# A hybrid SSD, attention and mixture-of-experts layer: group products moved ahead of attention, half as many partition sums, both ends of the expert stage rearranged

## The reference

```
cb     = einsum("bclgn,bcsgn->bcgls", cc, bc)            # C.B, one product per group
scores = cb[:, :, :, None] * decay                       # decay = exp(a_cs[l] - a_cs[s]), causal
y      = einsum("bcgrls,bcsgrp->bclgrp", scores, xdt) + d_skip * xs
yg     = y * silu(z)
yg     = yg * rsqrt(mean(yg * yg over the 512 columns of a group) + EPS) * norm_w
```

```
h = h + (g_ssd * y_ssd @ w_ssd_out + g_mla * y_mla @ w_o) @ w_out
h = h + moe_ffn(rms_norm(h))          # top 4 of 32 experts, clamped SwiGLU, 1024 -> 2048 -> 1024
out = rms_norm(h)[:, 16:]
```

## Time and profile before

| | |
|---|---|
| median of 3 runs (lowest, highest) | 1380.6 us (1380.5, 1382.89) |
| the profiled execution: time, span | 1382.37, 1380.6 us |
| mean granted TensorE clock | 0.994 of full |
| TensorE busy, weight loads | 1319.2 us (96%), 637.0 us (46%) |
| VectorE, ScalarE, GpSimd busy | 457.8, 319.6, 73.3 us |
| moved by DMA | 461.83 MB, mean 335 GB/s |
| dense part, join, SSD loop | to 191, to 199, to 282 us |
| gates and output products, routing | to 394, to 441 us |
| experts, tail behind the last weights | to 1364, to 1380.6 us |

### The profile page before, as it was taken

How to read it: one execution, slowest core, us unless ns; L and a number is a source line. 1 busy time by engine, 2 the same in 40 slices (tenths; PEclk the granted TensorE clock), 3 DMA queues, 4 the chain that set the end, 5 groups by cost and what they waited for, 6 DMA issues and landing times.

```text
span 1380.6 us, 18645 instructions
## 1 busy us (share of the span) xinstructions
PE 1319.2 (96%) x7121; PEld 637.0 (46%) x7121; DVE 457.8 (33%) x1185; ACT 319.6 (23%) x649; POOL 73.3 (5%) x83
## 2 busy tenths in 40 slices
PE   7999999999999999999999999999999999999995
PEld 5858888899964333333322222222222223333331
DVE  5838879888523211121111121111112111121112
ACT  3537767654311111011100110110010011111001
POOL 0000004422211000000000000000000000000000
PEclk9999999999998999999999999999999999999999
DMA  6333133334976999999999999999999999999995
GB/s 247 132 122 122 62 123 122 123 144 181 375 318 226 420 417 416 417 418 418 418 418 418 417 416 419 419 418 418 417 417 417 418 415 418 418 418 418 417 416 225
DMA packets 77426, 461.83 MB, mean 335 GB/s; under 512 B 6864, under 2 KB 6864, under 8 KB 41152
## 3 DMA queue, kind: packets, MB, share of 16 engines
q1 hardware_dynamic: 76624, 458.67, 82.0%
q0 software_dynamic: 752, 2.49, 0.5%
HBM read 460.09 MB, written 1.05 MB: 334 GB/s over the span
## 4 chain that ended last, share of the span: by engine, by line
PE 66%; SPq 18%; DMA 12%; issue 2%; DVE 1%; ACT 1%; ACTq 0%; DVEq 0%
PE bank L1308 62%; DMA ring<-w_dram 12%; SPq L407 9%; SPq L374 8%; PE bank L1643 1%; PE bank L1637 1%; DMA ring<-slabs_dram 1%; PE bank L1659 1%; PE bank L1505 1%; PE bank L1427 0%; DVE split L889 0%; SPq L395 0%; PE bank L1447 0%; PE bank L1443 0%; PE bank L1444 0%
## 5 line engine op out<-in xcount | busy, mean ns | idle before, releaser
L1308 PE MATMUL bank<-ring,work 128*64 128x512 f32 (+5 forms) x2264 | 551.7, 593 | 34.5 <-DMA ring<-w_dram 31.8
L1308 PE MATMUL bank<-work 128*64 128x512 f32 (+8 forms) x2200 | 431.2, 546 | 6.5 <-issue 2.2
L1308 PEld LDWEIGHTS bank<-ring,work 128*64 128x64 f32 (+2 forms) x2264 | 175.2, 141 | 361.0 <-issue 266.6
L1308 PEld LDWEIGHTS bank<-work 128*64 128x64 f32 (+4 forms) x2200 | 145.2, 143 | 259.2 <-issue 245.6
L1256 DVE COPY work<-bank 128x256 f32<-128x256 f32 x32 | 13.6, 425 | 495.9 <-PE bank L1659 495.9
L1308 PE MATMUL bank<-hn_hi,split 128*128 128x256 f32 (+1 forms) x896 | 172.9, 288 | 0.0
L1308 PEld LDWEIGHTS bank<-hn_hi,split 128*128 128x128 f32 x896 | 141.4, 189 | 0.6
L1308 PE MATMUL bank<-hn_lo,split 128*128 128x256 f32 (+1 forms) x448 | 127.3, 284 | 0.0
L1230 DVE TENSOR_SCALAR work<-bank 128x256 f32<-128x256 f32 x64 | 24.2, 419 | 275.5 <-PE bank L1308 275.5
L889 DVE TENSOR_TENSOR split<-ring,split 128x1024 fp32r<-128x1024 f32 x80 | 99.7, 1248 | 27.2 <-ACT split L547 26.8
L742 ACT ACTIVATE work<-bank 128x512 f32<-128x512 f32 x32 | 19.1, 598 | 333.3 <-PE bank L1308 333.3
(11 more groups left out here) (250 smaller groups left out, 909.7 us busy)
## 6 DMA issues: line engine op xcount, KB each, us to landing
ring<-w_dram SPq DMA_DIRECT2D x256, 1024.0 KB, 21.6
work<-w_dram SPq DMA_DIRECT2D x128, 1024.0 KB, 20.1
ring<-slabs_dram SPq DMA_DIRECT2D x23, 2048.0 KB, 7.4
ring<-slabs_dram SPq DMA_DIRECT2D x2, 1152.0 KB, 5.2
ring<-slabs_dram SPq DMA_DIRECT2D x1, 1536.0 KB, 12.0
ring<-slabs_dram SPq DMA_DIRECT2D x1, 1280.0 KB, 8.7
work<-x_dram POOLq DMA_DIRECT2D x2, 512.0 KB, 16.0
out_dram<-work SPq DMA_DIRECT2D x4, 256.0 KB, 2.5
```

The costliest lines, as they stand in the source:

```text
L1308: return pe.matmul(o, lhsT, rhs, start=start, stop=stop)
```

## The change

Seven edits, on five engines. (1) The group products stand between query units 2 and 3, their masking on VectorE ahead of the rotation of the queries, and `CBm` lies elsewhere; the SSD loop starts without them, the rows and transposes of chunk 1 come behind unit z 1, and ScalarE reads z 0 ahead of the loop. (2) The squares of two chunks are added on VectorE (`ysum_of`), and `gsum_of` runs on the sums, 8 times. (3) Logits are made in halves; the transposes of the third part of h1 stand ahead of the rest of the last `w_out` part, one copy of h1 ahead of the last half of the logits; the normalizer takes the first half's sum ahead of time. (4) The bias products of `up` stand on their own (`up_bias`), ahead of the wait for the gathered rows; in expert 0 they stand ahead of its transposes, behind the wait for the count. (5) For the last expert the transposes stand inside `down` of the one before, and `down` uses another bank and buffer with the scatter inside. (6) TensorE, ScalarE read the count ahead of their last expert's work; the branch stays in its place. (7) The stores of the second block are issued by ScalarE.

```diff
-        CBm = w(R + 4096, GROUPS * DECAY).rearrange("p (g t) -> p g t", g=GROUPS)
+        CBm = w(7424, GROUPS * DECAY).rearrange("p (g t) -> p g t", g=GROUPS)
...
-        ysq = w(R + 11008, 512).rearrange("p (i t) -> p i t", i=2)
+        ysq = w(R + 4096, 1024).rearrange("p (i t) -> p i t", i=4)
...
+        scat_last = w(13312, SEQ)
+        actT_last = xgT
...
         @block.sync
-                sp.wait_ge(y1_ready, n + 1)
-                sp.dma_start(out[P:2 * P, n * 512:(n + 1) * 512], fin[:, 1, n * 512:(n + 1) * 512]).then_inc(y_out, 16)
...
         @block.scalar
             def squares_of(c):
                 a.wait_ge(y2_ready, c + 1)
-                if c >= 2:
-                    a.wait_ge(gsum_done, c - 1)
-                a.activation(ysq[:, c % 2, :], y2T[:, c, :], ACT.Square, scale=0.5).then_inc(ysq_ready, 1)
+                if c >= 4:
+                    a.wait_ge(gsum_done, c // 2 - 1)
+                a.activation(ysq[:, c % 4, :], y2T[:, c, :], ACT.Square, scale=0.5).then_inc(ysq_ready, 1)
...
+            z_of(0)
             for c in range(NX):
                 if c + 1 < NX:
                     diff2_of(c + 1)
                 if c:
                     squares_of(c - 1)
...
+                    z_of(c)
                 if c + 1 < NX:
                     exp_decay(c + 1)
                 hi_of(PZ + c + 3)
...
             xn_copy(0, 1)
+            xn_copy(1, 0)
             top_weights(0)
             square_half(1, 1)
-            xn_copy(1, 0)
             xn_copy(1, 1)
...
+            a.wait_ge(count_ready, 1)
             expert_round(FIRST)
-            a.wait_ge(count_ready, 1)
-            cm = a.value_load(cmax_i[0:1, 0:1], min_val=0, max_val=SEQ)
-            with a.If(cm > SLOTS):
+            with a.If(cm[0] > SLOTS):
...
+            for n in range(2):
+                a.wait_ge(y1_ready, n + 1)
+                a.dma_start(out[P:2 * P, n * 512:(n + 1) * 512], fin[:, 1, n * 512:(n + 1) * 512]).then_inc(y_out, 16)
...
         @block.vector
+            for g in range(GROUPS):
+                cb_of(g)
+
             d.wait_ge(proj_read, U["q", 7] + 1)
...
+            def ysum_of(c):
+
+                d.wait_ge(ysq_ready, c + 1)
+                d.tensor_tensor(ysq[:, c % 4 - 1, :], ysq[:, c % 4 - 1, :], ysq[:, c % 4, :], ALU.add).then_inc(ysum_ready, 1)
...
             sc_of(0)
+            lo_of(PZ + 2)
             for c in range(NX):
                 if c + 1 < NX:
                     diff_of(c + 1)
                     xdt_of(c + 1)
-                lo_of(PZ + c + 2)
+                if c:
+                    lo_of(PZ + c + 2)
...
-                if c and c % CHUNKS_PER_GROUP == 0:
+                if c % 2 == 0 and c:
+                    ysum_of(c - 1)
+                if c > CHUNKS_PER_GROUP and c % CHUNKS_PER_GROUP == 1:
                     var_group(c // CHUNKS_PER_GROUP - 1)
+            ysum_of(NX - 1)
...
+            def first_half(b):
+                d.wait_ge(h1_squared, 2 * b + 1)
+                link(d.tensor_scalar(ssh[:, b:b + 1], ssh4[:, b, 0:1], 0.5 / D, 0.5 * EPS, ALU.mult, ALU.add))
+
             def rstd_block(b):
                 d.wait_ge(h1_squared, 2 * (b + 1))
-                link(d.tensor_tensor(ssh[:, b:b + 1], ssh4[:, b, 0:1], ssh4[:, b, 1:2], ALU.add))
-                rstd_col(rsh[:, b:b + 1], ssh[:, b:b + 1], D, EPS, rsn_ready)
+                link(d.scalar_tensor_tensor(ssh[:, b:b + 1], ssh4[:, b, 1:2], 0.5 / D, ssh[:, b:b + 1], ALU.mult, ALU.add))
+                rsqrt_col(rsh[:, b:b + 1], ssh[:, b:b + 1], rsn_ready)
...
         @block.tensor
+            def chunk_products():
+                pe.wait_ge(conv_fin, 8)
+                pe.wait_ge(kpeT_ready, 2)
+                for g in range(GROUPS):
+                    ps = bank[4 + g]
+                    for (t0, n), (lo, at) in zip(BLOCKS, DECAY_AT):
+                        last = mm(ps[0:n, at:at + SEQ - lo], BT[:, g, t0:t0 + n], CT[:, g, lo:SEQ])
+                    last.then_inc(cb_done, 1)
...
                     last.then_inc(proj_done, 1)
+                    if i == 2:
+                        chunk_products()
...
-            pe.wait_ge(pv_read, KD)
-            for g in range(GROUPS):
-                ps = bank[4 + g]
-                for (t0, n), (lo, at) in zip(BLOCKS, DECAY_AT):
-                    last = mm(ps[0:n, at:at + SEQ - lo], BT[:, g, t0:t0 + n], CT[:, g, lo:SEQ])
-                last.then_inc(cb_done, 1)
...
+            def gsum_of(i):
+
+                pe.wait_ge(ysum_ready, i + 1)
+                if i and i % 2 == 0:
+                    pe.wait_ge(gsum_read, i // 2)
+                mm(bank[7][:, 0:SEQ], ones[:, :], ysq[:, i % 2 * 2, :], i % 2 == 0, i % 2 == 1).then_inc(gsum_done, 1)
...
             for c in range(NX):
-                if c + 1 < NX:
+                if 0 < c < NX - 1:
                     acum_of(c + 1)
                     xtr_of(c + 1)
...
+                if c == 0:
+                    acum_of(1)
+                    xtr_of(1)
+                    pe.wait_ge(pv_read, KD)
...
-                if c:
-                    gsum_of(c - 1)
+                if c >= 3 and c % 2:
+                    gsum_of(c // 2 - 1)
...
             wout_unit(1, 1, range(0, 3))
-            logits(0)
+            logits(0, 0)
+            logits(0, 1)
+            h1_transposes(1, 0)
             wout_unit(1, 1, range(3, KD)).then_inc(wout_done, 1)
-            h1_transposes(1, 0)
+            logits(1, 0)
             h1_transposes(1, 1)
-            logits(1)
...
             keep_h1(0, 0)
+            logits(1, 1)
             keep_h1(0, 1)
...
+            def up_bias(t):
                 pe.wait_ge(bsel_ready, t + 1)
...
                     pe.wait_ge(up_read, t + 1)
+                    up_bias(t + 1)
                     up(t + 1, pair, odd, between)
...
+                    if gathers:
+                        down(t)
+                    else:
+                        pe.wait_ge(scat_ready, t + 1)
+                        down(t, between=lambda: last_transposes(t + 1))
...
                 gather(t0)
-                gather_trans(t0)
...
                     pe.wait_ge(bias_in, 64)
                     pe.wait_ge(count_ready, 1)
+                up_bias(t0)
+                gather_trans(t0)
                 up(t0, pair0, 0, first_between)
...
-                act_transposes(t0 + E - 1)
-                scatter(t0 + E - 2)
-                hot_transposes(t0 + E - 1)
-                down(t0 + E - 1)
+                if r is FIRST:
+                    cm.append(pe.value_load(cmax_i[0:1, 0:1], min_val=0, max_val=SEQ))
+                pe.wait_ge(up_read, t0 + E)
+                down(t0 + E - 1, 4, actT_last, lambda: scatter(t0 + E - 2))
...
-            with pe.If(cm > SLOTS):
+            with pe.If(cm[0] > SLOTS):
```

128 lines of the change are left out of this document (71 added, 57 removed).

## The result

The changed kernel takes **1372.23 us** in the median (1372.12 to 1372.85, four runs); the kernel before, on the same chip, 1380.59 (1380.5 to 1382.89). The ratio is 0.9935, with a 95% interval of 0.9922 to 0.9947: 8.4 us faster, where 6.9 were forecast. The two profiled executions lie 9.5 us apart (1382.37 and 1372.85, spans 1380.6 and 1371.1).

The account below looks back on a forecast made before the run. The expert weight stream was taken to bound the kernel, movable only in its start and the tail behind it. Terms 1.1 + 3.5 + 1.4 + 0.9 = 6.9 us off the 1380.6 median gave 1373.7 us, range 1368.5 to 1378.0.

Parts of the forecast that it names:

- C: Routing before expert 0: positions start 3.5 us earlier, 3.35 left, less 1.95 for a slower gather: 1.4 us won.
- rival (a): Routing and expert 0: the granted clock stays up through gather and first k step, worth 5.0, total 1370.2; chance 0.25.
- What bounds the kernel: Expert weight stream, 447 to 1362 us at 417 GB/s: only its start and the tail behind it can move.
- A: Join of attention and SSD: moving the C·B products removes waiting around them, 1.1 us won, bounds 0 and 1.9.
- The sign given for it: SSD loop: the unit of chunk 2 would start about 3.1 us later than now (4.16 - 1.1).
- B: SSD loop: eight partition sums fewer save TensorE 5.0 us, VectorE takes back 1.5: 3.5 us won, bounds -1.2 and 5.0.
- VectorE becomes the slower of the two: SSD loop: VectorE needs 5.15 us a chunk, TensorE 4.96; 0.19 a chunk, 2.5 us over some 13 chunks.
- Rival (b): SSD loop: VectorE takes back all that the eight sums gave, total 1377.2; chance 0.14.
- rival (d): SSD loop: VectorE's additions wait in a ring through ScalarE and TensorE, 12.4 us lost, total 1386.1; chance 0.04.
- I expect the lower level on the gather: Expert 0: after a TensorE wait the clock falls on the gather, which goes from 1.94 to 3.9 us.
- D: Tail behind the last weights: count read earlier, so the branch starts 0.9 earlier: 0.9 us won, bounds 0.2 and 1.9.
- The stores on ScalarE and the steps between experts: Outputs issued by ScalarE: 0, within 0.3 us; bias products ahead of the gathered rows' wait between experts: nothing.

Follow-up runs that it names:

- more_adds: The changed kernel with four more unread VectorE additions of squares ahead of each of its eight real ones: median 1383.5 us.
- before_fill: The kernel before, with eight unread matrix products put into TensorE's two waits of the routing stage: median 1380.5 us.
- no_ends: The changed kernel with the first expert's order, the count's read, the last expert's transposes and bank, and ScalarE's stores as before: median 1374.3 us.
- no_routing: The changed kernel with the routing stage in the old order, the first expert's order left as changed: median 1377.0 us.
- near_scatter: The changed kernel with TensorE's last scatter in a branch of its own ahead of the one that skips the further rounds: median 1372.8 us.
- no_products_move: The changed kernel with the C·B products, their masking, the tanh order of z and the SSD loop's start as before: median 1376.5 us.

## Why the prediction was right, point by point

The total held (1373.7 forecast, 1372.2 measured, inside 1368.5 to 1378.0), but with one term far off, one close by luck and the others close. The parts of the profiled pair come to 10.65 us, not 6.9. That the medians show 8.4 of them has two causes outside the argument: the changed kernel was 1.17 us late from its first stretch, and the two profiled executions stand 1.8 and 0.6 us above their medians. The range held C's error because it was drawn to take in rival (a).

- **What bounds the kernel: right.** The stream moved with its first reload and kept its rate.
- **A, 1.1 forecast: 1.05 measured**, and 1.06 when undone. The sign given for it, a unit of chunk 2 that starts 3.1 us later, contradicts the term: by its own numbers it starts at 191.43 + 4.16 + 7.20 = 202.79, which is 1.1 earlier than 203.93. It came 1.05 earlier behind the latent transposes.
- **B, 3.5 forecast: 3.5 in the profiled pair** (4.0 in the loop and 0.3 of sums behind it, less the wait of 0.77). In six further profiles with the additions, a second wait near 272 us (0.24 to 0.73) and slightly longer loops leave 2.2 to 2.8, so that the exact 3.5 is luck: of the seven, that profile has the fewest long masked decays. The forecast put the meetings with GpSimd into its lower bound only (at each addition); in these profiles they come at the masked decay, and their number goes with the price. The step "VectorE becomes the slower of the two" was right in its effect and wrong in its place: no wait for it is in the loop, which ran at 4.98 us a chunk, against 4.96 by the forecast's sum for TensorE. The backlog shows at the loop's end, where VectorE also has the roots to make. Rival (b) was the same mechanism, carried too far; rival (d) didn't appear: more_adds, with 1.7 us of additions for two chunks, is the only kernel that ends near the time of before.
- **C, 1.4 forecast: 6.0 measured.** The step that failed is "I expect the lower level on the gather": the gather ran at 2.4 GHz, and so did everything through the first k step. That is rival (a), priced at 5.0. Term by term: positions 4.45 (3.5 forecast), gather no slower (-1.95 forecast), first k step 1.25 (nothing forecast), between the positions and the k step 0.3 (-0.15 forecast for the count's wait). The forecast got the positions' 3.5 us by putting the copies at 2.4 GHz, and didn't say how much of it is the clock. before_fill shows that it is three quarters of what was measured: the positions end 4.45 us sooner behind the logits after the change (the second block's mask products start 12.62 behind, against 17.07: 435.58, right behind the row of 435.21, less 418.51), and 3.35 of that is there with the old order and the fill (13.72).
- **D, 0.9 forecast: 0.8 by the means** of all profiles, 0.1 in the profiled pair, where the stream of the changed kernel happened to be slower. By the wait behind ScalarE's copy it is 0.7 in the pair (1.53 and 0.82) and 1.0 by the means (1.78 and 0.81). The branch took 3.75 us, not 3.4.
- The stores on ScalarE and the steps between experts: nothing, as forecast. From the last scatter's start to the end it is 11.9 us before and after, and in no_ends; the stream has 417 GB/s in both.
- The chances: 0.86 for faster is a little high by their own sum, 0.50 + 0.25 + 2/3 of 0.14 = 0.84.

The terms of the profiled pair add up: 1.05 + 3.5 + 6.0 + 0.1, less the 1.17 that the changed kernel was late by from its first stretch, is 9.5. Without any fall of the clock the parts are worth 1.05 + 2.2 to 3.5 + 1.0 + 0.8, or 5 to 6.4 us; the rest is the clock.

**Open:** what decides in an execution whether the clock falls. The old order fell in both of its profiles without a fill, the new one in one of eleven, and the runs without a profile give only a mean clock. On one chip it was 0.995 to 0.997 in all eight executions of no_routing (old order) and 0.997 or 0.998 in near_scatter (new order), but 0.996 in four of seven of no_products_move (new order too). So the order bears on it and doesn't settle it. Where it fell in those was not seen.

## What to carry to other kernels

Price a stretch of small dependent steps at both levels of the clock: here an order that shortens TensorE's waits from 1.16 to 0.55 us was worth 1.0 us by itself and 5.0 more by the clock. Where an edit moves work to a second engine that is nearly full, look for the bill behind the loop, at the next place where that engine has extra to do. And put what is urgent on TensorE in the near body of a branch: its branch over the further rounds took 3.3 to 4.0 us, one into the next instructions 0.08.

## What the runs showed of the hardware

- A compare-and-branch of TensorE took 3337 to 3980 ns in the fourteen profiles when it skipped the further rounds, and 78 ns when its body followed, in the four programs that have both. The other engines skipped theirs in 50 to 67 ns.
- With eight small products in two waits of 0.42 and 1.16 us, the granted clock was 1.00 over the following 6 us in the profiled execution, where it was 0.50 without them. The means of the other ten executions, 0.994 to 0.997 against 0.998, say that this was not so, or not everywhere, in them.
- The new order of the routing ran with a clock of 1.00 in ten profiles and fell to 0.50 in an eleventh (means of 0.78, 0.50 and 0.87 over three stretches of 2 us, or some 3.4 us at the lower level by our estimate from them), at a price of 1.55 us.
- VectorE's product of 128x832 took 1.02 or 1.55 us in nearly all chunks of the changed kernel and its relatives, and GpSimd's of 128x256 beside it from 1.13 to 2.25. The long form came 8 times in 16 in one profile of the changed kernel and 11 times in the other, and 14 times with the additions on GpSimd.
